# Last stage of a decoder step on one core: the bias row added by TensorE for 12 tiles and by VectorE from PSUM for five, the sample tile first, reciprocals per three tiles

## What is computed

```python
def _layer_norm(x, g, b):
    mu = jnp.mean(x32, -1, keepdims=True)
    var = jnp.mean(jnp.square(x32 - mu), -1, keepdims=True)
    y = (x32 - mu) * lax.rsqrt(var + LN_EPS) * g + b
...
    y_moe = _hier_moe(u2, w_group, b_group, w_route, b_route, w_gate, w_up, w_down)
    x = _layer_norm(ALPHA * x + (1.0 + g2[:, None]) * y_moe, ln2_g, ln2_b)
```

## Time and profile before

| | us |
|---|---|
| median of three runs | 1376.2 (1374.5 to 1378.71) |
| the profiled execution | 1375.88 |
| its span in the profile | 1374.0 |
| last product of TensorE to the end of the span | 1284.9 to 1374.0 |
| first load of the last stage | 1294.19 |
| first multiplication by ln2_g on POOL | 1302.99 |
| issue of the last store | 1370.71 |

### The profile page before, as it was taken

How to read it: one execution, slowest core, us unless ns; L and a number is a source line. 1 busy time by engine, 2 the same in 40 slices (tenths; PEclk the granted TensorE clock), 3 DMA queues, 4 the chain that set the end, 5 groups by cost and what they waited for, 6 DMA issues and landing times.

```text
span 1374.0 us, 23129 instructions
## 1 busy us (share of the span) xinstructions
PE 1128.7 (82%) x6461; PEld 939.0 (68%) x6462; DVE 925.1 (67%) x1839; ACT 536.2 (39%) x915; POOL 546.0 (40%) x545
## 2 busy tenths in 40 slices
PE   5789999999989369999997069999999999999300
PEld 1278998899879348777875057777787787888200
DVE  2585988898887676555655866665775666543398
ACT  0445344534453412222222115544664565433242
POOL 1411202220222435555563424445565554444365
PEclk9789999999999689999997579999999999999755
DMA  9603213321322543344342358778897887554572
GB/s 348 232 19 144 70 52 122 122 68 54 122 76 65 180 151 124 123 147 143 137 138 100 107 172 246 205 207 235 245 284 228 233 242 208 131 123 92 160 291 114
DMA packets 106187, 215.04 MB, mean 157 GB/s; under 512 B 18091, under 2 KB 67759, under 8 KB 103187
## 3 DMA queue, kind: packets, MB, share of 16 engines
q1 hardware_dynamic: 85004, 163.14, 34.1%
q0 software_dynamic: 20736, 50.89, 16.7%
q10 hardware_dynamic: 415, 0.63, 0.1%
HBM read 153.93 MB, written 85.96 MB: 175 GB/s over the span
## 4 chain that ended last, share of the span: by engine, by line
PE 57%; DVE 22%; issue 6%; DMA 5%; ACT 4%; DVEq 2%; SPq 2%; ACTq 1%; POOL 1%; POOLq 0%
PE bank L1565 16%; PE bank L1567 15%; PE bank L1566 15%; PE bank L1516 4%; DVE arena L1189 2%; DMA ada_arena<-in_w_ada 2%; PE bank L1640 2%; DVE st L1480 1%; DVE arena L1497 1%; DVE arena L1212 1%; PE bank L1586 1%; ACT parts L884 1%; PE bank L1545 1%; DVE parts L1046 1%; DVE parts L1397 1%
## 5 line engine op out<-in xcount | busy, mean ns | idle before, releaser
L1565 PE MATMUL bank<-parts 128*128 128x256 f32 (+2 forms) x1616 | 569.3, 352 | 42.1 <-POOL parts L587 21.0
L1567 PE MATMUL bank<-parts 128*128 128x256 f32 (+2 forms) x1616 | 552.8, 342 | 0.0
L1566 PE MATMUL bank<-parts 128*128 128x256 f32 (+2 forms) x1616 | 552.2, 342 | 0.0
L1565 PEld LDWEIGHTS bank<-parts 128*128 128x128 f32 x1616 | 308.9, 191 | 88.9 <-issue 26.5
L1567 PEld LDWEIGHTS bank<-parts 128*128 128x128 f32 x1616 | 308.0, 191 | 35.4
L1566 PEld LDWEIGHTS bank<-parts 128*128 128x128 f32 x1616 | 308.8, 191 | 31.8
L1516 PE MATMUL bank<-ident,arena 128*128 128x128 f32 (+3 forms) x792 | 120.8, 286 | 36.3 <-DVE arena L1212 18.3
L1516 PEld LDWEIGHTS bank<-ident,arena 128*128 128x128 f32 (+3 forms) x792 | 95.9, 148 | 67.6 <-issue 24.4
L565 POOL TENSOR_TENSOR arena<-arena 128x256 f32<-128x256 f32 (+1 forms) x36 | 26.0, 724 | 285.3 <-DVE h_last L1127 154.7
L1397 DVE TENSOR_TENSOR parts<-arena,parts x90 | 104.8, 1219 | 18.5 <-ACT parts L884 18.5
L909 ACT ACTIVATE arena<-bank,w_now 128x512 f32<-128x512 f32 x96 | 66.1, 689 | 125.6 <-PE bank L1567 72.9
(11 more groups left out here) (266 smaller groups left out, 1579.6 us busy)
## 6 DMA issues: line engine op xcount, KB each, us to landing
arena<-in_w_gate SPq DMA_DIRECT2D x16, 1024.0 KB, 5.8
arena<-in_w_up SPq DMA_DIRECT2D x16, 1024.0 KB, 10.1
arena<-in_w_down SPq DMA_DIRECT2D x16, 1024.0 KB, 13.3
arena<-in_w_ada SPq DMA_DIRECT2D x14, 1024.0 KB, 5.9
ada_arena<-in_w_ada SPq DMA_DIRECT2D x8, 1024.0 KB, 16.7
arena<-in_x_prompt SPq DMA_DIRECT2D x8, 1024.0 KB, 7.0
yT_d<-arena SPq DMA_DIRECT2D x16, 512.0 KB, 4.2
arena<-yT_d SPq DMA_DIRECT2D x16, 512.0 KB, 4.8
```

Of the source, the lines that this page charges most:

```text
L1565: pe.matmul(out, x_hi, w_hi, start=start, stop=False)
L1566: pe.matmul(out, x_hi, w_lo, start=False, stop=False)
L1567: return pe.matmul(out, x_lo, w_hi, start=False, stop=stop)
```

## The change

The last stage handles the tiles in the order 16, 0, 1, ..., 15; q is the place in that order. Places 2, 5, 8, 11 and 14 form FIN_DVE, the other 12 form FIN_PE.

- SP waits for `ys0`, `ys1` and also `yr0`, `yr1` before any load, then loads the two `y_pair` halves, the sample tile and the rest, with at most three tile loads under way (NZ = 3 in place of 6).
- DVE takes the statistics of three tiles, then one reciprocal of three columns and three TENSOR_SCALAR (mean times 1/sd times -1, the 1/sd read as a scalar operand) in place of SCALAR_TENSOR_TENSOR. Groups are places 0; 1 to 3; 4 to 6; ...; 13 to 15; 16. ACT takes one square root of three columns for each group.
- ACT writes `ln2_b` into PSUM banks 0 and 1, ahead of its last evacuation in the last expert slot.
- POOL multiplies by `ln2_g` as before.
- For FIN_DVE tiles DVE adds `ln2_b` out of banks 0 and 1 in two instructions of 512 columns, six places later.
- For FIN_PE tiles TensorE copies the tile into a pair of PSUM banks by a product with the identity and adds a product of a row of ones with the row `ln2_b`: four products of 512 columns of type f32 for each tile, in three pairs of banks in turn. ACT copies both halves back into the tile, four places behind its `norm_z`.
- SP stores a tile after `fo_ok` (DVE) or `fo_act` (ACT).

```diff
-            for t in range(NT - 1):
-                if t == 13:
-                    for b in range(2):
-                        sp.wait_ge(S[f"yr{b}"], 16 * (SLOTS // 2))
-                if t >= NZ:
-                    sp.wait_ge(z_in[t % NZ], 16 * (t // NZ))
-                sp.dma_start(zt[t], x1_t[t]).then_inc(z_in[t % NZ], 16)
+            for b in range(2):
+                sp.wait_ge(S[f"yr{b}"], 16 * (SLOTS // 2))
             for k in range(2):
                 sp.dma_start(y_pair[k][0:NS, :], ysamp_d[k * NS:(k + 1) * NS, :]).then_inc(pair_in, 16)
+            for q, t in enumerate(FIN_TILES):
+                if q >= NZ:
+                    sp.wait_ge(z_in[q % NZ], 16 * (q // NZ + 1 - 1))
+                dst, src = (zt[t], x1_t[t]) if t < NT - 1 else (zt[t][0:NS, :], z_d[SEQ:NTOK, :])
+                sp.dma_start(dst, src).then_inc(z_in[q % NZ], 16)
...
+            def roots_z(i, lo, hi):
+                act.wait_ge(S["fvar_ready"], hi)
+                act.activation(sd_z[:, lo:hi], mv_z[:, lo:hi, 1], ACT.Sqrt).then_inc(S["fsd_ready"], 1)
...
+            def out_z(q, t, n=P):
+                m = FIN_PE.index(q)
+                act.wait_ge(S["fb_mm"], m + 1)
+                for h in range(2):
+                    act.activation(zt[t][0:n, 512 * h:512 * h + 512], bank[2 + 2 * (m % 3) + h][0:n, :],
+                                   ACT.Copy).then_inc(S["fo_act"], 1)
+
+            for i, (lo, hi) in enumerate(FIN_GROUPS):
+                roots_z(i, lo, hi)
+                for q in range(lo, hi):
+                    norm_z(q, FIN_TILES[q], P if FIN_TILES[q] < NT - 1 else NS)
+                    if q - FIN_PE_LAG in FIN_PE:
+                        out_z(q - FIN_PE_LAG, FIN_TILES[q - FIN_PE_LAG], P if FIN_TILES[q - FIN_PE_LAG] < NT - 1 else NS)
...
+            def f_scales(i, lo, hi):
+                dve.wait_ge(S["fsd_ready"], i + 1)
+                o.step(dve.reciprocal(rs_z[:, lo:hi, 0], sd_z[:, lo:hi]))
+                for q in range(lo, hi):
+                    dve.tensor_scalar(rs_z[:, q, 1:2], mv_z[:, q, 0:1], rs_z[:, q, 0:1], -1.0,
+                                      ALU.mult, ALU.mult).then_inc(S["frs_ready"], 1)
...
+            for i, (lo, hi) in enumerate(FIN_GROUPS):
+                for q in range(lo, hi):
+                    f_stats(q, FIN_TILES[q], P if FIN_TILES[q] < NT - 1 else NS)
+                    if q - FIN_LAG in FIN_DVE:
+                        f_out(q - FIN_LAG, FIN_TILES[q - FIN_LAG])
+                f_scales(i, lo, hi)
...
+            def add_bias(q, t, n=P):
+                m = FIN_PE.index(q)
+                pe.wait_ge(S["fg_ok"], q + 1)
+                if m >= 3:
+                    pe.wait_ge(S["fo_act"], 2 * m - 4)
+                for h in range(2):
+                    cols = slice(512 * h, 512 * h + 512)
+                    out = bank[2 + 2 * (m % 3) + h][0:n, :]
+                    pe.matmul(out, ident[0:n, 0:n], zt[t][0:n, cols], start=True, stop=False)
+                    last = pe.matmul(out, ones[0:1, 0:n], ln2_b[0:1, cols], start=False, stop=True)
+                last.then_inc(S["fb_mm"], 1)
```

More of the change, by code:

```diff
@@ L37 @@
 LN_EPS = 1e-5
-NZ = 6
+FIN_TILES = (16, *range(16))
+FIN_GROUPS = ((0, 1), (1, 4), (4, 7), (7, 10), (10, 13), (13, 16), (16, 17))
+FIN_DVE = (2, 5, 8, 11, 14)
+FIN_PE = tuple(q for q in range(17) if q not in FIN_DVE)
+FIN_LAG, FIN_PE_LAG = 6, 4
+NZ = 3
 LRU_C = 8.0
@@ L268, in build @@
             fin_in fin_s_in dump_in g2_in wgt_ok hotw_ready wslot_mm dst_ok yr0 yr1 w_now_ok fvar_ready fsd_ready frs_ready fnorm
-            fg_ok fo_ok fo_stored""".split()}
-        z_in = [sem(f"z_in{n}") for n in range(NZ)]
+            fg_ok fb_ready fb_mm fo_act fo_ok fo_stored""".split()}
+        z_in = [sem(f"zin{n}") for n in range(NZ)]
         pair_in = sem("pair_in")
@@ L941, in _, with norm_z @@
             hT_evac(s)
+            act.wait_ge(S["fin_in"], 32)
+            act.wait_ge(S["xT_lo_ok"], 2 * SLOTS)
+            for h in range(2):
+                act.activation(bank[h][:, :], ln2_b[:, 512 * h:512 * h + 512], ACT.Copy).then_inc(S["fb_ready"], 1)
             y_evac(s, 1, SLOTS // 2 - 1)
[L945 to L958, removed]
+            def roots_z(i, lo, hi):
+                act.wait_ge(S["fvar_ready"], hi)
+                act.activation(sd_z[:, lo:hi], mv_z[:, lo:hi, 1], ACT.Sqrt).then_inc(S["fsd_ready"], 1)
+            def norm_z(q, t, n=P):
+                act.wait_ge(S["frs_ready"], q + 1)
+                act.activation(zt[t][0:n, :], zt[t][0:n, :], ACT.Identity, bias=rs_z[0:n, q, 1:2],
+                               scale=rs_z[0:n, q, 0:1]).then_inc(S["fnorm"], 1)
+            def out_z(q, t, n=P):
[10 more added lines that the diff above has]
+                        out_z(q - FIN_PE_LAG, FIN_TILES[q - FIN_PE_LAG], P if FIN_TILES[q - FIN_PE_LAG] < NT - 1 else NS)
+            for q in range(NT - FIN_PE_LAG, NT):
+                if q in FIN_PE:
+                    out_z(q, FIN_TILES[q], P if FIN_TILES[q] < NT - 1 else NS)
         @block.vector
@@ L1485, in f_stats @@
+                dve.tensor_scalar(mv_z[0:n, q, 1:2], mv_z[0:n, q, 1:2], LN_EPS / (ALPHA * ALPHA), None,
                                   ALU.add).then_inc(S["fvar_ready"], 1)
[L1487 to L1492, removed]
@@ L1494, in f_out @@
-            def f_out(t, n=P):
-                dve.wait_ge(S["fg_ok"], t + 1)
-                dve.tensor_tensor(zt[t][0:n, :], zt[t][0:n, :], ln2_b[0:n, :], ALU.add).then_inc(S["fo_ok"], 1)
-            dve.wait_ge(S["fin_in"], 32)
[L1500 to L1508, removed]
@@ L1509, in _, with f_out @@
-            f_out(NT - 1, NS)
+            def f_scales(i, lo, hi):
[4 more added lines that the diff above has]
+                                      ALU.mult, ALU.mult).then_inc(S["frs_ready"], 1)
+            def f_out(q, t, n=P):
+                dve.wait_ge(S["fg_ok"], q + 1)
+                for h in range(2):
+                    dve.tensor_tensor(zt[t][0:n, 512 * h:512 * h + 512], zt[t][0:n, 512 * h:512 * h + 512], bank[h][0:n, :],
+                                      ALU.add).then_inc(S["fo_ok"], 1)
@@ new lines, in _ @@
+            o.step(dve.memset(mv_z[:], 1.0))
+            dve.wait_ge(S["fin_in"], 32)
+            dve.wait_ge(S["fb_ready"], 2)
+            for i, (lo, hi) in enumerate(FIN_GROUPS):
[4 more added lines that the diff above has]
+                f_scales(i, lo, hi)
+            for q in range(NT - FIN_LAG, NT):
+                if q in FIN_DVE:
+                    f_out(q, FIN_TILES[q])
@@ L1828, in _ @@
             down(s)
+            def add_bias(q, t, n=P):
[3 more added lines that the diff above has]
+                    pe.wait_ge(S["fo_act"], 2 * m - 4)
+                for h in range(2):
+                    cols = slice(512 * h, 512 * h + 512)
[3 more added lines that the diff above has]
+                last.then_inc(S["fb_mm"], 1)
+            for q in FIN_PE:
+                add_bias(q, FIN_TILES[q], P if FIN_TILES[q] < NT - 1 else NS)
 CHUNK_STEPS = 58
```

26 lines of the change are left out of this document (13 added, 13 removed).

## The result

The changed kernel takes 1411.63 us (median of four runs, 1403.36 to 1413.54) against 1375.78 (four runs, 1374.5 to 1378.71) for the kernel before: a ratio of 1.0252, 95% interval 1.0213 to 1.0291. It is 36 us slower where I had forecast 14 us faster. This is the first rival, and a harder form of it than I had priced.

A forecast was written before the change was run, and what follows sets the result against it. The last stage was taken as bound by a ring of DVE's held instruction, ACT and POOL. Engines' end 1355.9 plus 3.3 to the span's end gave 1359.2, rounded to 1360, set at 1362 us against the runs; range 1357 to 1371.

The forecast's parts named there:

- the first rival: Last stage, TensorE: clock stays at 1.2 GHz, twelve tiles at 6.9 us, span 1396.4, time 1399 us; chance 0.11.
- The ring of 1491, ACT and POOL: Last stage before: DVE's line 1491 held until POOL ends, then ACT 1.24, POOL 2.35; 3.72 us a tile.
- The unknown costs on DVE: Last stage beside POOL: scaling taken as 0.15 us (other end 6 us in all), PSUM additions unheld (other end 6.5 us).
- the second rival: Last stage: DVE or POOL still held by additions or scalings, 6 to 6.5 us more, time 1368; chance 0.10.
- The start: Last stage's beginning: first load issued at 1294.7, DVE starts at 1299.6, normalization until 1306.9, POOL until 1309.3.
- The clock: Last stage, TensorE: first tile 5.6 us from a 1.2 GHz start, then full clock at 3.44 us a tile.
- The price of a product: TensorE's f32 products, two instructions each: 0.43 us apart at full clock, 0.86 at 1.2 GHz; a tile 3.44 or 6.9.
- the eleven tiles from 1314.9: Last stage's middle: TensorE by itself needs 37.8 us for 11 tiles, until 1352.7.
- The engines' balance: Last stage at full clock: the four engines need 6.2 to 7.0 us for three tiles, where 11.1 was taken before.
- a tenth of a us for each hand-over: Last stage, POOL and TensorE chains: twelve hand-overs of 0.1 us put the end at about 1354.7.

The follow-up runs named there:

- e7: Kernel before with one edit, TENSOR_SCALAR with a scalar operand in place of SCALAR_TENSOR_TENSOR for the mean: 1371.57 us (ten runs), ratio 0.9994.
- e4: Changed kernel with all 17 tiles getting their row from DVE out of PSUM, none from TensorE: 1358.97 us (nine runs), ratio 0.9916.
- e1: Changed kernel with the bias product reading ln2_b from 128 rows (identity times ln2_b) in place of one row of ones: 1356.0 us, single execution.
- e10: Changed kernel with the identity products left out, only the one-row products kept: 1362.38 us, single execution.
- e8: Changed kernel with 40 f32 products of 128 rows put ahead of TensorE's first tile: 1412.03 us, single execution.
- e9: Kernel of e1 with 32 f32 products of 128 rows put ahead of TensorE's first tile: 1357.71 us (four runs), ratio 0.9915.
- e1_again: Same kernel as e1, run several times beside the kernel before: 1358.19 us (five runs), ratio 0.9905.
- e6: Kernel of e1 with 28 f32 products of 128 rows put ahead of TensorE's first tile: 1358.86 us (four runs), ratio 0.9902.
- e11: Kernel of e1 with the sample tile fourth, its wait and pair loads just ahead of its own load: 1357.29 us (four runs), ratio 0.99.
- e3: Kernel of e1 with the tile itself as loaded operand in both products in place of the identity: 1358.45 us, single execution.
- e2: Changed kernel with the bias products left out, TensorE only copying tiles through the identity: 1356.41 us, single execution.
- e5: Changed kernel with 28 f32 products of 128 rows put ahead of TensorE's first tile: 1410.02 us, single execution.

## Why the prediction was wrong

**What bounds the kernel before: right.** The ring of 1491, ACT and POOL is the bound. e7 shows that a second bound lies only 0.26 us a tile below it, DVE's own work and the order of its list, and e4 and e1 that with both gone, and the rest of the change in place, the stage shrinks by 12 us.

**The unknown costs on DVE: right.** Scaling 0.205, addition 0.68 each, never held, so the second rival did not come: one element was not held as sixteen had been. The scaling's 0.15 was 0.05 too little, which nothing waits for.

**The start: 2.3 us too early.** The first load was issued at 1295.16, I had 1294.7. DVE's first addition was 6.5 us after it (1301.67), I had 4.9. What failed here is the landing: 3.7 us was that of a first load with nothing ahead of it, here 768 KB in three transfers came together, and the sample tile landed 5.0 us after its issue. POOL's first multiplication stood at 1309.23 in place of 1306.9.

**The clock: the step that failed.** I priced TensorE's tiles at 3.44 us from the second on, taking from the earlier trace rows that unbroken f32 products bring the clock up. Those had 128 rows. The first rival named what was different, "half of them have one row of ones as operand", and then I argued against it with the same rows, which had no such product: a row of another form carried the term of the sum, and I gave 0.11 to the case that it would not carry. The runs in its place: one-row products leave the clock at 0.50 with TensorE busy for 25.00 of 25.00 us (e10), and as half of the mix they let it fall from 1.00 with no pause (e8); 128-row products in their place bring it to 1.00 (e1) and hold it (e9). Why the chip grants so little clock to one-row products no run shows.

**The price of a product: the second term.** The rival said 6.9 us a tile and 1399. It was 8.0. (Its 0.86 for an instruction at 0.50 is right, 1.71 a product in e1_again, but it does not follow from "seven in 4.0 us", which would be 0.57: those counts include instructions that the window's edges cut.) At 0.50, the chain that ended last shows pairs of rows 2.00 us long for every product of 128 columns, in e1_again 1.71 as long as the loaded operand stays the same, and 2.00 once, at the change from 64 to 128 rows:

```profile
1307.91 1.71 PE bank L1865 x2
1309.62 2.00 PE bank L1864 x2
1311.62 1.71 PE bank L1865 x2
```

So each change of the loaded operand costs 0.29 us at this clock, and the change made one at every product. Over 12 tiles that is 48 x 0.29 = 14 us at most; the chain itself took 95.8 us where the rival had 82.6, so 13.2. The working closes: the rival's span 1396.4, plus 13.2 for the alternation, plus 2.3 for the start, is 1411.9, and 1411.6 was measured. Taken from the forecast's side: TensorE's chain was 45.4 us long in the forecast (1309.3 to 1354.7) and 95.8 in the trace, which is 50 of the 51.6 us between the two spans; some 13 of the 50 are the alternation at the low clock and the rest the clock.

The forecast's own 3.44 us a tile was too low as well, clock or not. At 1.00 in e8 the change's products stood 1.00 apart in place of 0.86, so a tile would be 4.0 and two of them 8.0, above POOL's 7.0 for three. By that the eleven tiles from 1314.9 would have ended near 1358.9 and not 1352.7. This is an estimate: with the clock up, the change would have come out some 5 us and the late start above the forecast, near 1370, with TensorE as the bound.

That the alternation costs the time by the operand's change, and not by the number of rows, is read from one such product in e1_again and was not tried by itself at either clock.

**The engines' balance: right for 128 rows.** In e1_again, POOL runs 16 multiplications with one gap of 0.83 us, and TensorE ends 6.5 us after it, by its cold start; in e9, warm, 4.9. The forecast had 3.5 and a tenth of a us for each hand-over. With the clock as I had assumed and one operand loaded throughout, the stage took 65.8 (e9) to 68.1 us (e1_again), and the forecast was 65.3. That nearness is partly luck: those kernels don't pay the alternation, and the change would have. One of the four timed runs of the change took 1403.36, 6.6 us under the next; no trace of it exists, and what differed there stays open.

The smallest edit that beats the kernel before is e1, one line of the change: 0.95% faster (0.62% to 1.28%), where the change was 2.5% slower. e4, e6, e9 and e11 gain as much, and the runs don't tell them apart.

## What to carry to other kernels

A busy TensorE is not yet one that runs at full clock: look at the granted clock of each stretch, and price a product by a row of its own form, the number of rows of the array and the change of the loaded operand included. A vector that is added through a product with a row of ones is cheaper from a tile in which it is already repeated over all partitions, if that tile is there. Where an engine in the middle of a chain copies for a slower one, the chain runs at the slowest one's pace, so the engine with the least known price should be tried alone first. Here the version without it (e4) gains as much as any.

## What the runs showed of the hardware

- One-row products (1 x 128 loaded in all but the first tile, 512 columns, f32) kept the granted clock at 0.50 through 25 us of unbroken work in e10. In the changed kernel a mix of one half did so for 95.8 us, and in e8 the clock fell from 1.00 under it. The Trainium skill, "TensorE: Matmul & The Clock Gate", section "What's actually happening", says that activity releases the throttle and describes it by how busy the engine has been recently. The trace agrees for 128-row products (e1, e11) and not for one-row ones, which were busy for 25.00 of 25.00 us at 0.50 (e10).
- Four products of 64 rows and 64 columns, 7.0 us without a pause, left the clock at 0.50 in e1_again; in e11, with 128 rows from the start, it rose after 3.5 us. At 1.00 the same 64-row tile left it there (e9).
- What is in the loaded operand, identity or dense numbers, made no difference to the clock (e1, e3).
- With the clock at 1.00, a pause of 0.67 us in e9 and one of 1.75 us in e2 left it there. Pauses of 1.76 us in e5 and 2.2 in e6 were followed by a fall to 0.50 within the next product, and it fell during two of 2.6 us in e2.
- f32 products of 512 columns: 0.86 us each at 1.00 and 1.71 at 0.50 with the same operand loaded; where each product loads another, 1.00 at 1.00 (e8, 64 columns loaded) and 2.00 at 0.50 (128 columns).
- Beside POOL's multiplication of two SBUF tiles, DVE's TENSOR_TENSOR with one input in PSUM (0.68 us) and its one-element TENSOR_SCALAR with a scalar operand (0.205) ran without a hold: 32 such additions in e4, 13 such scalings in e9.
